# Moving six of the sixteen final row tiles one expert earlier, with the rows that this expert changes done twice

## The reference, cut to what matters

```python
gate, idx = lax.top_k(jnp.swapaxes(aff, 1, 2), cap)      # cap = 256 tokens for each of 16 experts
xs = h[bidx, idx]
hid = jax.nn.silu(einsum(xs, w1)) * einsum(xs, w3)       # each 1024 x 1024
y = einsum(hid, w2) * gate[..., None]
x = x + m_lat[5] * zeros_like(h).at[bidx, idx].add(y)
return x * rsqrt(mean(x * x, axis=-1) + 1e-6) * final_norm_w
```

## Time and profile before

| | us |
|---|---|
| median of three runs (2230.57 to 2232.57) | 2232.33 |
| the profiled execution's own time | 2235.2 |
| its span | 2233.5 |
| TensorE matmul busy | 2122.0 (95%) |
| DVE busy | 1381.5 (62%) |
| ACT busy | 989.0 (44%) |
| POOL busy | 275.5 (12%) |
| mean granted clock of TensorE, share of full | 0.965 |

### The profile page before, as it was taken

How to read it: one execution, slowest core, us unless ns; L and a number is a source line. 1 busy time by engine, 2 the same in 40 slices (tenths; PEclk the granted TensorE clock), 3 DMA queues, 4 the chain that set the end, 5 groups by cost and what they waited for, 6 DMA issues and landing times. The chain is left out here.

```text
span 2233.5 us, 34798 instructions
## 1 busy us (share of the span) xinstructions
PE 2122.0 (95%) x13430; PEld 1851.2 (83%) x13430; DVE 1381.5 (62%) x2116; ACT 989.0 (44%) x1612; POOL 275.5 (12%) x336
## 2 busy tenths in 40 slices
PE   6999999999999799994799999999999999999995
PEld 4777888777777588883799999999999999999994
DVE  3663648995974676747556655566555665555657
ACT  5822544344622444420344444444444444444455
POOL 0000000000001010100102122111221112211120
PEclk6999999999999899995899999999999999999998
DMA  7473323333346655328347556575565765657656
GB/s 254 144 263 106 111 88 102 115 124 92 101 132 217 219 186 182 135 101 312 114 170 264 196 184 217 193 263 200 183 218 188 263 204 183 218 185 263 206 163 243
DMA packets 188284, 407.93 MB, mean 183 GB/s; under 512 B 15956, under 2 KB 53396, under 8 KB 187300
## 3 DMA queue, kind: packets, MB, share of 16 engines
q1 hardware_dynamic: 162068, 317.84, 41.2%
q0 software_dynamic: 26128, 88.92, 12.5%
HBM read 329.59 MB, written 77.12 MB: 182 GB/s over the span
## 5 line engine op out<-in xcount | busy, mean ns | idle before, releaser
L55 PE MATMUL bh<-xt_hi,shi 128*128 128x256 f32 x2048 | 581.2, 284 | 5.5 <-DVE slo L2224 5.5
L56 PE MATMUL bh<-xt_lo,shi 128*128 128x256 f32 x2048 | 580.9, 284 | 0.0
L57 PE MATMUL bh<-xt_hi,slo 128*128 128x256 f32 x2048 | 580.8, 284 | 0.0
L2224 DVE TENSOR_TENSOR slo<-raw,shi 128x1024 fp32r<-128x1024 f32 x384 | 455.9, 1222 | 159.0 <-ACT shi L2128 154.5
L2128 ACT ACTIVATE shi<-raw 128x1024 fp32r<-128x1024 f32 x384 | 388.7, 1050 | 127.3 <-PE eby L57 127.3
L55 PEld LDWEIGHTS bh<-xt_hi,shi 128*128 128x128 f32 x2048 | 394.5, 193 | 6.8 <-issue 6.1
L56 PEld LDWEIGHTS bh<-xt_lo,shi 128*128 128x128 f32 x2048 | 394.6, 193 | 0.6
L57 PEld LDWEIGHTS bh<-xt_hi,slo 128*128 128x128 f32 x2048 | 394.5, 193 | 0.0
L55 PE MATMUL bank<-h_hi,whi 128*128 128x512 f32 x704 | 286.2, 406 | 0.4 <-DVE wlo L708 0.4
L56 PE MATMUL bank<-h_lo,whi 128*128 128x512 f32 x704 | 278.6, 396 | 0.0
L57 PE MATMUL bank<-h_hi,wlo 128*128 128x512 f32 x704 | 278.2, 395 | 0.0
(11 more groups left out here) (334 smaller groups left out, 3147.9 us busy)
## 6 DMA issues: line engine op xcount, KB each, us to landing
raw<-in_exp_w_dram SPq DMA_DIRECT2D x96, 2048.0 KB, 11.3
uT<-stage POOLq DMA_DIRECT2D x72, 256.0 KB, 2.7
xb<-in_ada_w_dram SPq DMA_DIRECT2D x24, 512.0 KB, 5.7
wraw<-in_w_in_dram SPq DMA_DIRECT2D x22, 512.0 KB, 5.0
adaw<-in_ada_w_dram SPq DMA_DIRECT2D x8, 1024.0 KB, 10.0
xb<-in_x_dram SPq DMA_DIRECT2D x16, 512.0 KB, 4.5
xt<-in_x_dram POOLq DMA_DIRECT2D x16, 512.0 KB, 5.3
x2d<-xt POOLq DMA_DIRECT2D x16, 512.0 KB, 2.9
```

What stands on the lines that cost most here:

```text
L55: nc.tensor.matmul(out, w_hi, x_hi, start=start, stop=False)
L56: nc.tensor.matmul(out, w_hi, x_lo, start=False, stop=False)
L57: return nc.tensor.matmul(out, w_lo, x_hi, start=False, stop=stop)
L2224: nc.vector.tensor_tensor(item_dst(slo, n), item_src(n), item_dst(shi, n), ALU.subtract).then_inc(S["w_lo_ready"], 1)
```

## The change

Row work is now numbered by c from 0 to 17.

- c = 0 to 5: row tiles 0 to 5, done with `x2d` as it is after expert 13's sum, through three new 512 KB buffers `rb`, three tiles at a time. SP loads the first three in expert 14 once `scatter_over` is 14, behind K0 and K1 of expert 15, and stores them behind K2 and K3. Only then are the next three loaded. ACT squares c = 0 and 1 in step 4 of expert 14, 2 in step 5, 3 between items 21 and 22, and 4 and 5 between items 22 and 23. DVE works out two groups of roots in expert 14 (step 5, and after item 23) and multiplies c = 0, 1 in step 6, 2 in step 7, and 3, 4, 5 in steps 0, 2, 3 of expert 15.
- c = 6, 7: the 256 rows that expert 14 adds to. POOL gathers them from `x2d` by `sidx` into `yo` once expert 14's sum has landed, and writes them to the output by `sidx` when tiles 0 to 5 have been stored. All of these rows are done here, also those of tiles 6 to 15.
- c = 8 to 17: row tiles 6 to 15, three through `rb` and seven through the weight buffers of K0 and K1, loaded in one run when tiles 0 to 5 have been stored and `scatter_over` is 15. They are stored when the redone rows have been.
- Expert 14 leaves the hardware loop and is written out as expert 15 is (`kind` 1 and 2), and its `result` does both y tiles of expert 13 in step 1.

The core of the difference:

```diff
         def loop(eng, body):
-            body(0, True, False)
-            with eng.Fori(1, NE - 1) as e:
-                body(e, False, False)
-            body(NE - 1, False, True)
+            body(0, True, 0)
+            with eng.Fori(1, NE - 2) as e:
+                body(e, False, 0)
+            body(NE - 2, False, 1)
+            body(NE - 1, False, 2)
 # SP
-                sp.wait_ge(S["scatter_over"], NE - 1)
-                for t in range(NT):
-                    if t % 4 == 0:
-                        sp.wait_ge(S["w_lo_ready"], (NE - 1) * NI + last_item[RAW_ORDER[t // 4]] + 1)
-                    sp.dma_start(rows(t), v.x2d[t * P:(t + 1) * P, :]).then_inc(rows_loaded[t // 4], 16)
...
+                next_weights(NE - 1, RAW_ORDER[0])
+                next_weights(NE - 1, RAW_ORDER[1])
+                sp.wait_ge(S["scatter_over"], NE - 2)
+                for c in range(3):
+                    row_in(c)
+                next_weights(NE - 1, RAW_ORDER[2])
+                next_weights(NE - 1, RAW_ORDER[3])
+                for c in range(3):
+                    row_out(c)
+                sp.wait_ge(S["rows_stored"], 48)
+                for c in range(3, EARLY):
+                    row_in(c)
+                next_weights(NE - 1, RAW_ORDER[4])
+                next_weights(NE - 1, RAW_ORDER[5])
+                for c in range(3, EARLY):
+                    row_out(c)
+                sp.wait_ge(S["rows_stored"], 96)
+                sp.wait_ge(S["scatter_over"], NE - 1)
+                for c in range(REDO + 2, NC):
+                    if (c - REDO - 5) % 4 == 0:
+                        g = (c - REDO - 5) // 4
+                        sp.wait_ge(S["w_lo_ready"], (NE - 1) * NI + last_item[RAW_ORDER[g]] + 1)
+                    row_in(c)
+                sp.wait_ge(redo_stored, 32)
+                for c in range(REDO + 2, NC):
+                    row_out(c)
 # POOL
+                        if last:
+                            for i in range(3):
+                                pool.wait_ge(rb_loaded[i], 32)
...
+                for s in range(2):
+                    pool.indirect_dma_start(out=yo[s][:, :], out_offset=None, in_=v.x2d,
+                                            in_offset=bass.IndirectOffsetOnAxis(ap=sidx[s][:, :], axis=0)
+                                            ).then_inc(redo_loaded[s], 16)
...
+                pool.wait_ge(S["rows_stored"], 16 * EARLY)
+                pool.wait_ge(S["row_ready"], REDO + 2)
+                for s in range(2):
+                    pool.indirect_dma_start(out=v.out0[0], out_offset=bass.IndirectOffsetOnAxis(ap=sidx[s][:, :], axis=0),
+                                            in_=yo[s][:, :], in_offset=None).then_inc(redo_stored, 16)
 # ACT
                         split(e, 2 * f + 1)
+                        if kind == 1 and f in (4, 5):
+                            squares(*{4: (0, 2), 5: (2, 3)}[f])
                         if last and f >= FD - 3:
-                            squares(*{FD - 3: (0, 3), FD - 2: (3, 5), FD - 1: (5, 8), FD: (8, 10)}[f])
+                            squares(*{FD - 3: (6, 8), FD - 2: (8, 10), FD - 1: (10, 12), FD: (12, 14)}[f])
...
+                    if kind == 1:
+                        squares(3, 4)
                     split(e, 22)
+                    if kind == 1:
+                        squares(4, 6)
                     split(e, 23)
 # DVE
+                        if kind == 1 and f in (5, 6, 7):
+                            if f == 5:
+                                roots(0, 3)
+                            else:
+                                normal(*{6: (0, 2), 7: (2, 3)}[f])
+                        if last and f in (0, 2, 3):
+                            normal(*{0: (3, 4), 2: (4, 5), 3: (5, 6)}[f])
                         if last and f == FD - 2:
-                            roots(0, 4)
+                            roots(6, 9)
...
-                        if last and f == 1:
+                        if kind and f == 1:
...
-                        for i, (first, end) in enumerate([(4, 6), (6, 8), (8, 9), (9, 11), (11, 12), (12, 16)]):
+                        for i, (first, end) in enumerate([(9, 11), (11, 12), (12, 14), (14, 15), (15, 17), (17, 18)]):
                             split(e, 18 + i)
                             normal(first, end)
...
+                        if kind == 1:
+                            roots(3, 6)
```

118 lines of the change are left out of this document (77 added, 41 removed).

## The result

| | before | the change |
|---|---|---|
| median, us | 2232.45 (7 runs, 2230.57 to 2233.78) | 2242.01 (7 runs, 2239.84 to 2242.45) |
| ratio, 95% interval | | 1.0040 (1.0029 to 1.0052) |
| the profiled execution's own time / span | 2235.2 / 2233.5 | 2242.01 / 2239.8 |
| mean granted clock | 0.965 | 0.974 |

The change is slower by 9.6 us (0.4%), where 3.4 had been forecast. The time lies 1 us above the range, and the likeliest case, within 0.2%, was wrong.

A forecast was written before the change was run, and what follows sets the result against it. Expert 15 was taken as bound by row work on ACT and DVE, earlier experts by TensorE. Stall 7.6 + clock 2.9 + round trip 1.7 - expert 15's gain 8.8 = +3.4 us on 2232.3: 2235.7, range 2230 to 2241.

The forecast's parts named there:

- the likeliest case: Whole kernel: time stays within 0.2% of before, forecast 2235.7 us, own range 2231 to 2236.8; chance 0.47.
- Part 1: Expert 14, first three rows queued behind K0 and K1: TensorE stalls 7.6 us at item 10, slower clock costs 2.9.
- the rows pass the weights: Faster rival, expert 14: row loads overtake K0 and K1, so no stall at item 10; 2224.5 us, chance 0.07.
- K1 lands as late as before: Slower rival, expert 14: K1 lands 15.6 us after issue, stall 11.1, sum +6.9, 2239.2 us; chance 0.16.
- the estimate of a stall of 9.4 by 358 GB/s: Item 10 of expert 14: alternative at the skill's HBM rate, whole sum 1.8 higher; the prediction used 410 GB/s instead.
- Part 2: End of expert 14, next three rows through the buffers: small waits at items 23 and 0, together 1.7 us.
- The slower rival's mechanism: Buffer round trip becomes the bound: K2 and K3 take 3.6 us more, sum +7.0, 2239.3 us; chance 0.25.
- Part 3: Expert 15: gets back 8.8 us in step 5, steps 6 to 8 and the tail; bounds 5.5 and 9.5.
- Step 5: Expert 15: second gather lands at 2161.7 to 2162.8, silu at about 2163.4 instead of 2166.41.
- the stall of 2.56: TensorE's 2.56 us wait at item 12 of expert 15 in the profile before, claimed to be gone.
- steps 6 to 8: Expert 15: lead kept, ACT's 2.35 us row wait gone, last `hid` 5.3 us sooner, 2.3 of it here.
- the tail: After item 23 of expert 15: one row tile instead of four on DVE, 3.5 us gained.

The follow-up runs named there:

- e1: The change with SP waiting for expert 13's sum and loading the first three row tiles ahead of K0 and K1: 2233.20 us, ratio 1.0003.
- e6: The change with its own queue order, the early rows' squares two steps later, and their roots and tiles later too: 2230.56 us, ratio 0.9991.
- e2: e1 with the stores of c = 0 to 2 and the loads of c = 3 to 5 also ahead of K2 and K3: 2231.25 us, ratio 0.9994.
- e3: e2 with the stores of tiles 3 to 5 held until expert 14's sum has landed: 2227.78 us, ratio 0.9982.
- e7: e4 with the loads of tiles 6 to 15 held until the gathers of the redone rows have landed: 2227.02 us, ratio 0.9978.
- e10: The change with the loads of tiles 6 to 15 held until the gathers of the redone rows have landed: 2239.45 us, ratio 1.0035.
- e12: e1 with the loads of tiles 6 to 15 held until the redone rows have been gathered: 2231.40 us, ratio 0.9994.
- e8: The kernel before with expert 14 written out behind the hardware loop, nothing else changed: 2231.41 us, ratio 0.9996.
- e5: The kernel before with the multiplications of row tiles 13 to 15 behind item 23 left out: 2227.90 us, ratio 0.9983.
- e9: The kernel before, unchanged, profiled a second time: 2231.09 us, ratio 0.9999.
- e11: e3 with the loads of tiles 6 to 15 also held until the redone rows have been gathered: 2228.83 us, ratio 0.9986.
- e4: e2 with tiles 3 to 5 squared, multiplied and stored earlier, around the end of expert 14: 2231.31 us, ratio 0.9989.

## Why the prediction was wrong

**Part 1 was right**, in mechanism and in sum: the rows queue behind K0 and K1 (10.72 us of waiting for "some 10"), 8.4 of stall for 7.6 and 1.7 of clock for 2.9, 10.2 in all for 10.5. e1 and e6 show the cause. The rival that the rows pass the weights is out, and so is the one that K1 lands as late as before (a stall of 11.1): K1 landed 13.5 us after its issue, not 15.6. That the sum is this near is partly luck, since the stall was 0.8 larger and the clock 1.2 smaller than said, the latter below its own bound of 2. In the changed kernel DMA moved 402 to 411 GB/s from 2082 to 2090, so the estimate of a stall of 9.4 by 358 GB/s did not come. The Trainium skill, "HBM Reference", section "Specifications (TRN2)", says that a core streaming alone measures well above the per-core share, near 425 GB/s; the trace agrees, with less than that and well above 358.

**Part 2 was right in kind**, the size 2.6 for 1.7 (bounds 0 to 5); e2 shows that all of it is the round trip. The slower rival's mechanism, a K3 landing 3.6 us later, did not come: it landed 13.0 us after its issue.

**Part 3 is where it failed, in its first step, "Step 5".** It said: the second gather lands at 2161.7 to 2162.8, the silu comes 3.0 us sooner, "the stall of 2.56 is gone". Measured against the profile it was worked on, the silu came 0.9 later and the stall was 3.47. The term that was wrong is the gathers' issue time. They were put at POOL's old one, but in the changed kernel they are issued 2.75 us later, and the second 0.8 later still. 1.5 of the 2.75 is gone in e3, which has no stores beside the scatters (0.8 of it against e2), and 0.6 is a small POOL operation, below. The landing of 8.2 to 9.3 us taken from the earlier trace rows came out right (8.8 and 9.3), partly by luck: it was taken to hold for a gather alone as well, where a gather with nothing of SP's beside it takes 4.2 to 6.6 (e7, e10, e12; 5.2 and 5.4 in the kernel before). That SP's ten loads run beside the gathers was thus in the price but was not seen as a cost that could be avoided; e10, which holds them back, is 4.1 us shorter there. Part 3 had been bounded below at 5.5, for gathers that land 3 us late. The second was used 27.7 us after the silu of step 0, where 23.2 to 24.3 had been said, so 3.5 to 4.6 late, and 5.5 is what part 3 gave. But the prediction made no rival of this bound and gave it no chance.

**The second failure was the baseline.** The stall of 2.56 us that part 3 wanted to remove was largely that execution's own (0 to 0.84 in the three others). The profiled execution lay 2.9 us above the median; I subtracted this from the time, but kept in the sum a gain that was, for the larger part, these same us. Against the second profile of before, step 5 of the change loses 4.1 us, and the whole is 163.56 - 153.08 = 10.5, against e8 9.0, around the 9.6 of the medians; against the first profile it is only 7.3.

The miss of 6.2 us is thus: part 1 -0.3, part 2 +0.9, part 3 +3.3, baseline 9.6 - 7.3 = +2.3. The last is a remainder. 0.35 us of it lie outside the span: the time of an execution is 2.1 us longer than its span in all versions of the change, and 1.75 in before, e5, e8 and e9; why, nothing here shows.

**The rest of part 3 was right:** steps 6 to 8 gave 2.5 (2.3 said) and the tail 3.9 (3.5 said). The other versions gave the same, but for e10, e11 and e12, whose held loads cost up to 2.6 in steps 6 to 8, and for the tails of e4 (1.8), e10 and e12 (3.0 each).

**Which version is best.** The idea of the change is worth 4 to 5 us when SP's queue is put right (in e7 also the place of the squares, roots and tiles of c = 3 to 5). e7 (2227.02, ratio 0.9978, 0.9969 to 0.9987) and e3 (2227.78, 0.9982, 0.9973 to 0.9991) beat both the kernel before and the change; between those two the intervals do not decide.

**Open:** why the first eight loads of before started late in one of four profiles; what of e7's 23.92 us would remain with e6's order of squares, which was not tried together with it; what holds up a gather beside stores or loads, of which only the landing was measured; and what lets the clock fall in the last items.

## What to carry to other kernels

A row of one profile that a gain is to come from should be read in a second execution first, above all a DMA wait, and above all where the profiled execution is slower than the median: then the excess and the wait may be the same microseconds. A load put into a single queue is paid for by what stands ahead of it there, so small urgent transfers go ahead of large ones that have slack, or the work that needs them goes later. Where work is shifted to an earlier time, list for each chain that it now passes (scatter, then gather, then the squares) which transfers newly run beside it; here holding back loads that were not yet needed brought the silu that waits for them 2.2 to 4.1 us sooner in three versions, but a shorter run is beyond the noise only in e7, and in e12 most of the gain went back because the held loads then came late.

## What the runs showed that was not expected

- An indirect gather of 256 rows (two DMAs of 128) lands in 4.2 to 6.6 us with nothing of SP's beside it, and in 7.1 to 9.9 beside stores or loads of whole rows (5.5 where the loads began 0.5 us behind it). The adding scatters land in 6.2 to 7.3 us alone (before, e3, e7), and the second of them in 8.1 to 9.5 beside stores (the change 8.8, e1 8.4, e2 8.1, e6 9.5, e10 9.4, e12 9.2).
- A small operation of POOL (`epause`, an addition on one column) can take as long as DVE stays busy. POOL and then DVE, in the changed kernel at the start of expert 15:

```profile
2145.27 3.43 POOL L2062 TENSOR_TENSOR epause<-epause 128x1 f32<-128x1 f32 x1 [69.56 <-DVE sidx L2324]
...
2155.17 1.60 POOL L2062 TENSOR_TENSOR epause<-epause 128x1 f32<-128x1 f32 x1
```

```profile
2145.09 1.28 DVE L2339 SCALAR_TENSOR_TENSOR rb<-rb,f_rst,fw 128x1024 f32<-128x1024 f32 x1
2146.29 2.36 DVE L2303 TENSOR_TENSOR slo<-raw,shi 128x1024 fp32r<-128x1024 f32 x2
...
2154.39 2.35 DVE L2303 TENSOR_TENSOR slo<-raw,shi 128x1024 fp32r<-128x1024 f32 x2
```

  An operation on one column took 3.43 us and ended at 2148.70, when DVE's run of three operations ended (2148.65); the second took 1.60 and ended at 2156.77, DVE's pair at 2156.74. In the kernel before the same two took 0.18 and 0.99, the latter ending at 2144.10, between the two operations of DVE's pair (2142.84 to 2145.19); so it is not always the whole run that it takes. The later one delays the second scatter by 0.6 us, which is part of the loss in step 5. The Trainium skill, "GPSIMD Engine Reference", section "1. Specifications", says that GpSimd's path to SBUF is shared with VectorE and contended by DVE instructions with two SBUF inputs; these DVE operations have two, and the trace agrees.
- TensorE's granted clock fell to 0.50 in e4 among the last items, after stretches in which TensorE was busy for 2 to 3 of 4 us, and to 0.76 and 0.81 in two such stretches of e2 (2204 to 2212), though its longest wait there was under 2 us in both. e5, e6, e7, e8, e10 and e12 have stretches below 1.00 there too; the same order of instructions kept 1.00 in the change, in e1, in e3 and in e11. With it goes a tail that is 2.1 us longer in e4 and 0.9 in e10 and e12; in e2, e6 and e7 it cost nothing.
